# Four experts packed into three blocks of 96 slots each in a mixture-of-experts trunk kernel

## What is computed

```python
def hier_moe(h, w_rg, b_rg, w_re, b_re, w_gate, w_up, w_down):
    ...
    g_p, g_idx = lax.top_k(g_prob, 1)
    ...
    e_top, e_loc = lax.top_k(e_in, MOE_TOPK)
    e_w = jax.nn.softmax(e_top, axis=-1) * g_p
    e_id = g_idx * MOE_EXPERTS_PER_GROUP + e_loc
    ...
    def expert_block(args):
        xb, e = args
        return (jax.nn.silu(xb @ w_gate[e]) * (xb @ w_up[e])) @ w_down[e]

    ys = lax.map(expert_block, (xs, block_e)).reshape(n_slots, d)
    return jax.ops.segment_sum(ys * slot_w[:, None].astype(ys.dtype), slot_tok, num_segments=t)
```

## Time and profile before

| | |
|---|---|
| median of 3 runs | 2938.73 us (2933.47 to 2940.27) |
| the profiled execution | 2944.05 us |
| its span on the core | 2942.3 us |
| PE busy | 2503.1 us, 85% |
| DVE busy | 1228.1 us, 42% |
| ACT busy | 908.3 us, 31% |
| moved by DMA | 370.44 MB |
| mean granted TensorE clock | 0.921 of full |

### The profile page before, as it was taken

How to read it: one execution, slowest core, us unless ns; L and a number is a source line. 1 busy time by engine, 2 the same in 40 slices (tenths; PEclk the granted TensorE clock), 3 DMA queues, 4 the chain that set the end, 5 groups by cost and what they waited for, 6 DMA issues and landing times.

```text
span 2942.3 us, 30451 instructions
## 1 busy us (share of the span) xinstructions
PE 2503.1 (85%) x10356; PEld 1423.7 (48%) x10374; DVE 1228.1 (42%) x2854; ACT 908.3 (31%) x1878; POOL 195.6 (7%) x372
## 2 busy tenths in 40 slices
PE   5979999188999959999579899973889997899994
PEld 3464445155664635454335644451556645445452
DVE  4342266885551331111332514768755414211115
ACT  2131266654450201111112214765544401111112
POOL 0000021200000000000200000211000000100002
PEclk9989999599999979999779899996999997899996
DMA  6100011301000369999411001121010005699985
GB/s 222 40 29 24 32 35 38 95 2 44 1 1 9 121 254 362 369 361 371 167 59 49 7 24 38 40 81 41 2 44 1 10 22 208 243 357 371 364 305 193
DMA packets 105455, 370.44 MB, mean 126 GB/s; under 512 B 20754, under 2 KB 39912, under 8 KB 80744
## 3 DMA queue, kind: packets, MB, share of 16 engines
q1 hardware_dynamic: 91500, 318.41, 30.2%
q0 software_dynamic: 13824, 50.34, 4.5%
HBM read 304.42 MB, written 64.30 MB: 125 GB/s over the span
## 4 chain that ended last, share of the span: by engine, by line
PE 75%; DVE 13%; ACT 5%; issue 4%; DMA 1%; POOL 0%; ACTq 0%; DVEq 0%; SPq 0%; POOLq 0%
PE bank L1065 15%; PE bank L732 9%; PE bank L1082 8%; PE bank L1013 8%; PE bank L735 6%; PE bank L766 6%; PE bank L696 5%; PE bank L949 4%; PE bank L952 4%; PE bank L795 4%; PE bank L933 2%; ACT group_arena L1318 2%; PE bank L1026 1%; PE bank L1051 1%; DVE residual L2090 1%
## 5 line engine op out<-in xcount | busy, mean ns | idle before, releaser
L696 PE MATMUL bank<-ident,group_arena 128*128 128x128 f32 (+1 forms) x1200 | 201.1, 308 | 129.1 <-DVE group_arena L1537 59.8
L766 PE MATMUL bank<-group_arena 96*128 96x512 f32 (+7 forms) x384 | 165.7, 531 | 133.9 <-ACTq L1216 125.9
L732 PE MATMUL bank<-w_ring,normed_cols 128*128 128x260 f32 (+2 forms) x768 | 268.0, 511 | 0.6 <-PE bank L735 0.6
L696 PEld LDWEIGHTS bank<-ident,group_arena 128*128 128x128 f32 (+1 forms) x1200 | 149.8, 156 | 190.0 <-issue 96.1
L1082 PE MATMUL bank<-heads_cols,group_arena 128*128 128x512 f32 x512 | 231.8, 595 | 2.8 <-DVE group_arena L2050 2.8
L1065 PE MATMUL bank<-w_ring,group_arena 128*128 128x512 f32 x512 | 229.5, 602 | 3.3 <-issue 1.7
L1065 PE MATMUL bank<-normed_cols,group_arena 128*128 128x512 f32 x512 | 224.9, 592 | 0.0
L1013 PE MATMUL bank<-w_ring,heads_cols 128*128 128x512 f32 x512 | 222.6, 594 | 2.0 <-DVEq L251 2.0
L732 PEld LDWEIGHTS bank<-w_ring,normed_cols 128*128 128x128 f32 x768 | 147.0, 192 | 120.0 <-issue 112.6
L1604 DVE TENSOR_REDUCE softmax_stats<-bank 128x1 f32<-128x128 f32 (+7 forms) x192 | 145.5, 758 | 122.7 <-PE bank L771 105.6
L2050 DVE COPY group_arena<-bank 128x256 f32<-128x256 f32 x64 | 27.2, 425 | 395.3 <-PE bank L1072 395.3
(11 more groups left out here) (326 smaller groups left out, 3479.8 us busy)
## 6 DMA issues: line engine op xcount, KB each, us to landing
heads_cols<-in_expert_w_down SPq DMA_DIRECT2D x64, 1024.0 KB, 9.0
w_ring<-in_expert_w_gate SPq DMA_DIRECT2D x32, 1024.0 KB, 10.0
w_ring<-in_expert_w_up SPq DMA_DIRECT2D x32, 1024.0 KB, 14.5
normed_cols<-in_expert_w_gate SPq DMA_DIRECT2D x32, 1024.0 KB, 10.5
normed_cols<-in_expert_w_up SPq DMA_DIRECT2D x32, 1024.0 KB, 15.1
expert_rows<-group_arena SPq DMA_DIRECT2D x64, 512.0 KB, 9.2
w_ring<-in_w_in SPq DMA_DIRECT2D x6, 2048.0 KB, 8.3
expert_rows<-heads_cols SPq DMA_DIRECT2D x1, 8192.0 KB, 28.7
```

Source lines behind the costliest of these rows:

```text
L696: last = pe.transpose(bank(4 + r % 2)[0:rows, col:col + src.shape[0]], src, ident[0:src.shape[0], 0:src.shape[0]])
L732: m = pe.matmul(proj_bank(n)[:, 0:width], HT[:, k, part * P:(part + 1) * P], w, start=(k == 0), stop=(k == K - 1))
L766: m = pe.matmul(L[:, c0:c1], a["q"](h, t), a["k"](h, c0, c1), start=True, stop=not (by_choice or diagonal))
```

## The change

The slots per expert go from 128 to CAP = 96, and they no longer own a block each: four experts (a quad) fill three blocks of 128 slots. PACKED = 24 blocks replace 32. `PIECES` says which rows of each of the three blocks belong to which expert of the quad, in pieces of 64 or 32 rows at multiples of 32. `gate_up` and `down` make one matmul per piece: its stationary operand is 64 or 32 columns wide, and its output goes to the PSUM partitions of the piece. All pieces of a block write the same bank. The further blocks become OVER = 21 and take whole experts (`WHOLE`).

A slot no longer holds a token alone but a row (choice x 1024 + token). It is computed as that row minus 2048, so that an empty slot, 0, becomes row 2048, which lies outside both tables and is skipped. POOL gathers with that index and scatters the results with an indirect store to `ys_dram`, which has 2048 rows; the store by SP in slot order is gone, and so is the filling of `ys_dram` in setup. At the end SP brings the rows back with 16 plain loads of 512 KB, where POOL gathered them before. `xg`, `xgT`, `sg`, `av`, `aT` and `yb` have three buffers in place of two, and the gate/up banks are three.

```diff
+CAP = 96
+PACKED = EXPERTS * CAP // P
+MORE = (SEQ - CAP + P - 1) // P
+OVER = N_ASSIGN // (CAP + 1)
...
+NB = PACKED // QUADS
+PIECES = [[(0, 0, 64), (0, 64, 32), (1, 96, 32)],
+          [(1, 0, 64), (2, 64, 64)],
+          [(2, 0, 32), (3, 32, 32), (3, 64, 64)]]
+WHOLE = [(0, 0, P)]
...
-            sp.wait_ge(setup_zero, 1)
-            sp.dma_start(ys_dram[EXPERTS * P:, :].rearrange("(a p) d -> p a d", p=P),
-                         YT[:, 0:1, :].to_broadcast([P, SLOT_ROWS - EXPERTS, D])).then_inc(setup_dma2, 16)
...
-                        settled(sp, gu_done, e + 1)
-                        load_gu(e + NW, w)
-                        settled(sp, dn_done, e + 1)
-                        load_dn(e + NW, w)
-                        store_y(e, w % 2)
+                def quad_of(q, first=False, last=False):
+
+                    e, w0 = q * NB, q * NW
+                    if not last:
+                        settled(sp, gu_done, e + 1)
+                        load_gu(w0 + NW, 0)
+                    if not first:
+                        settled(sp, dn_done, e)
+                        load_dn(w0 + 2, 2)
+                        load_dn(w0 + 3, 3)
+                    if not last:
+                        settled(sp, gu_done, e + 2)
+                        load_gu(w0 + NW + 1, 1)
+                        settled(sp, dn_done, e + 1)
+                        load_dn(w0 + NW, 0)
+                    if not last:
+                        settled(sp, gu_done, e + 3)
+                        load_gu(w0 + NW + 2, 2)
+                        load_gu(w0 + NW + 3, 3)
+                        settled(sp, dn_done, e + 2)
+                        load_dn(w0 + NW + 1, 1)
...
+                for s in range(NB):
+                    sp.wait_ge(y_out[s], 16 * QUADS)
+                for t in range(T):
+                    for k in range(2):
+                        sp.dma_start(back[k][:, t, :],
+                                     ys_dram[k * SEQ + t * P:k * SEQ + (t + 1) * P, :]).then_inc(back_in[t], 16)
...
+                for e in range(PACKED + NB):
+                    if e < PACKED:
+                        if e >= NB:
+                            pool.wait_ge(x_turned, e - NB + 1)
+                        gather(idx_i[:, e:e + 1], e, e % NB)
+                    if e >= NB:
+                        pool.wait_ge(y_lo, e - NB + 1)
+                        pool.wait_ge(y_hi, e - NB + 1)
+                        scatter(to_i[:, e - NB:e - NB + 1], e - NB, e % NB)
...
                     for k in range(K):
-                        m = pe.matmul(bank(2 + s)[:, :], xgT[:, s, k, :], Wgu[w][:, :, k, :], start=(k == 0), stop=(k == K - 1))
+                        for w, at, rows in pieces:
+                            m = pe.matmul(gu_bank[s][at:at + rows, :], xgT[:, s, k, at:at + rows], Wgu[w][:, :, k, :],
+                                          start=(k == 0), stop=(k == K - 1))
...
                     for h in range(2):
                         for k in range(2):
-                            m = pe.matmul(bank(6 + h)[:, :], aT[:, s, k, :], Wd[w][:, k, h * HALF:(h + 1) * HALF],
-                                          start=(k == 0), stop=(k == 1))
+                            for w, at, rows in pieces:
+                                m = pe.matmul(bank(6 + h)[at:at + rows, :], aT[:, s, k, at:at + rows],
+                                              Wd[w][:, k, h * HALF:(h + 1) * HALF], start=(k == 0), stop=(k == 1))
...
-                chain(dve.tensor_copy(idx_i, bank(2)[:, 0:SLOT_ROWS]))
+                chain(dve.tensor_scalar(to_f, bank(2)[:, 0:SLOT_ROWS], float(N_ASSIGN), None, ALU.add))
+                chain(dve.tensor_scalar(from_f, to_f, float(SEQ), -float(SEQ), ALU.is_ge, ALU.mult))
+                chain(dve.tensor_tensor(idx_i, from_f, to_f, ALU.add))
+                chain(dve.tensor_copy(to_i, to_f))
                 dve.sem_inc(idx_ready, 1)
```

More of the change, by code:

```diff
@@ L224, in trunk @@
         tile_root = sem("tile_root")
-        xg_in = [sem("xg_in0"), sem("xg_in1")]
+        xg_in = [sem(f"xg_in{i}") for i in range(NB)]
         gu_in = [sem(f"gu_in{i}") for i in range(NW)]
@@ L239, in trunk @@
         y_hi = sem("y_hi")
-        y_out = [sem("y_out0"), sem("y_out1")]
+        y_out = [sem(f"y_out{i}") for i in range(NB)]
         back_in = [sem(f"back_in{t}") for t in range(T)]
@@ L1073, in turn_a, with down @@
                     m.then_inc(a_turned, 1)
-                def down(e, w, s, n):
+                def down(e, pieces, s, n):
                     pe.wait_ge(a_taken, e + 1)
-                    pe.wait_ge(dn_in[w], 16 * n)
+                    for w in sorted({w for w, _, _ in pieces}):
+                        pe.wait_ge(dn_in[w], 16 * n)
                     wait_later(pe, y_lo, e)
@@ L1089, in quad_of @@
                 def quad_of(q, first=False, last=False):
-                    for w in range(NW):
-                        e, s, nx = q * NW + w, w % 2, q * 2 + ((w + 1) // 2 + 1)
-                        gate_up(e, w, s, q + 1)
-                        finish = not (first and w == 0)
+                    for r in range(NB):
+                        e, s, behind = q * NB + r, r, (r - 1) % NB
+                        gate_up(e, PIECES[r], s, q + 1)
+                        finish = not (first and r == 0)
                         if finish:
-                            turn_a(e - 1, 1 - s)
-                        if not (last and w == NW - 1):
-                            turn_x_lo(e + 1, 1 - s, nx)
-                            turn_x_hi(e + 1, 1 - s)
+                            turn_a(e - 1, behind)
+                        if not (last and r == NB - 1):
+                            turn_x_lo(e + 1, (r + 1) % NB, q + (r + 1) // NB + 1)
+                            turn_x_hi(e + 1, (r + 1) % NB)
                         if finish:
-                            down(e - 1, (w - 1) % NW, 1 - s, q + 1 if w else q)
+                            down(e - 1, PIECES[behind], behind, q + 1 if r else q)
                 quad_of(0, first=True)
@@ L1449, in quad_of @@
                 def quad_of(q, first=False, last=False):
-                    for w in range(NW):
-                        e, s = q * NW + w, w % 2
-                        gate(e, s)
-                        if not (last and w == NW - 1):
-                            take_x(e + 1, 1 - s)
-                        if not (first and w == 0):
-                            take_y(e - 1, 1 - s, q * 2 + (w - 1) // 2)
+                    for r in range(NB):
+                        e = q * NB + r
+                        gate(e, r)
+                        if not (last and r == NB - 1):
+                            take_x(e + 1, (r + 1) % NB)
+                        if not (first and r == 0):
+                            take_y(e - 1, (r - 1) % NB, q if r else q - 1)
                 quad_of(0, first=True)
@@ L1461, in _ @@
                 quad_of(QUADS - 1, last=True)
[L1462 removed]
+                take_y(PACKED - 1, NB - 1, QUADS - 1)
                 act.wait_ge(idx_ready, 1)
@@ L2059, in quad_of @@
                 def quad_of(q, first=False, last=False):
-                    for w in range(NW):
-                        e, s = q * NW + w, w % 2
-                        if not (first and w == 0):
-                            take_a(e - 1, 1 - s)
-                        gated(e, s)
-                        if not (last and w == NW - 1):
-                            take_x(e + 1, 1 - s)
-                        if not (first and w == 0):
-                            take_y(e - 1, 1 - s, q * 2 + (w - 1) // 2)
+                    for r in range(NB):
+                        e, behind = q * NB + r, (r - 1) % NB
+                        if not (first and r == 0):
+                            take_a(e - 1, behind)
+                        gated(e, r)
+                        if not (last and r == NB - 1):
+                            take_x(e + 1, (r + 1) % NB)
+                        if not (first and r == 0):
+                            take_y(e - 1, behind, q if r else q - 1)
                 quad_of(0, first=True)
```

159 lines of the change are left out of this document (74 added, 85 removed).

## The result

The changed kernel takes 3217.24 us (3214.19 to 3218.76), the kernel before 2939.5 us on the same chip. The ratio is 1.0947, 95% interval 1.0928 to 1.0966: 278 us slower. The forecast was 3236 us.

What follows compares the result with a forecast made beforehand. PE and DMA both bound the expert loops; after the change PE would. Loops +264, layer 0's further block +31, layer 1's way back +2, the rest 0: 2938.7 + 297 = 3236 us, range 2830 to 3265 (own case 3190 to 3265).

Steps and rivals of the forecast that it cites:

- The step and the block: Expert loops on PE: each 64/32 change empties the array; mixed step 2.00 us, mixed block 25.2, equal-piece block 11.8.
- The quad: Four experts in three blocks on PE: 62.2 us against 45.7 now, +132 us per layer, +264 in all.
- the tails: From last y to combine: +31 us in layer 0 for one further block, +2 us in layer 1.
- DMA: Expert loops after the change: DMA needs 40.1 of a quad's 62.2 us at 366 GB/s and is hidden.
- both limits hold at once: Middle of the expert loops before the change: PE busy 102.00 of 102 us, DMA share 1.00 at 366 GB/s.
- rival (a): Expert loops: sizes 64, 32 and 32 stream together, DMA bounds at 40.1 us per quad; 2850 us, chance 0.36.
- (b): Expert loops: only two streams run at once, quad 45.6 us; 2972 us, chance 0.06 together with (d).
- (c): Expert loops: no overlap of column pieces at 512 columns, 93 us per quad; 3724 us, chance 0.02.
- rival (d): Expert loops: skipped rows still cost DMA time, 46 us per quad where DMA bounds; near 2972 us, chance 0.06 with (b).
- DVE's walk: End of layer 1: DVE's empty iterations, not the gathers, are late; six more cost 3 to 5 us.
- POOL's stores: Gathers and scatters issued by POOL, 2 to 3 us per block: nothing, up to 5 us per quad if scatters are dearer.
- small edits: Routing's three more DVE steps, +0.6 us per layer, and setup without its clearing, -1 us: together 0.

Runs made afterwards that it cites:

- split rows: The kernel before with each gate_up and down matmul made of row pieces: 2960.59 us for 64 and 64, 3814.04 us for 64, 32 and 32.
- the other order: The changed kernel with the 64-wide piece of each quad's third block put first at every step: 3233.48 us.
- all-32 kernel: The changed kernel with every piece 32 columns wide, four per block: 2817.77 us, ratio to the kernel before 0.9578.
- the fuller gather: The changed kernel with all pieces 32 wide and half of gate_up's steps, its gather also moving a row for each empty slot: 2798.79 us.
- half of gate_up: The changed kernel with all pieces 32 wide, gate_up making only four of its eight steps: 2784.84 us.

## Why the prediction came out right

**The step and the block** carried the sum, and they hold. That 64 to 32 empties the array was a choice from neighbouring rows, at a chance of 0.55; no row of the kernel before had such a change, and the experiments with equal pieces and with split rows now show it. A step was to be 2.00 us; it is 1.985. Of my 0.15 and 0.13 us per change, the trace has 0.14 (0.093 and 0.051) at the 64-wide piece and 0.12 (0.093, 0.025 and the 7 ns between the two starts) at the 32-wide ones. A block with mixed pieces in both operations and no help at a seam is 25.15 us (kernel before with 64, 32 and 32), where I had 25.2; the block of equal pieces is 11.77, where I had 11.8.

**The quad** was 62.2 us by the prediction and is 60.97. The term that I had left out is the seam: 32-wide pieces at the end of down and at the start of gate_up stream together. With the other order, and without that overlap, it is 62.07. The two loops therefore cost 243 us in place of 264, 21 us less; the tails took 3 us more than said, and the parts of the profile make 1 us more than the medians differ by. That is the error of 19 us.

**DMA** was hidden, as I had said, at a share of 0.57 (I had written 0.65). But its limit was wrong. I read a share of 1.00 at 366 GB/s as "both limits hold at once". 366 was only what 11.43 us per expert ask for; at the same share of 1.00 the all-32 kernel moves 419. This had no part in the forecast, but it did in rival (a), whose 2850 us would have been 2818: its bound of 40.1 us per quad should have been 36 or less.

**Rival (a)**, the streams of all sizes together, is what the kernel with equal pieces does and the changed one does not. Rivals (b) and (c) fall with the periods. Of rival (d), the fuller gather speaks against a skipped row that costs its full time; whether it costs half of it or nothing stays open, and in the forecast, where PE bounds, it has no part.

**The tails.** Layer 0: 43 us between the last y and combine predicted, 44.07 measured, by the steps that I had listed; from the loop's last y to the y of the further block it was 25.4 us, as the steps' sum, and SP's loads came 12.9 us behind the scatter. Layer 1: 12 to 17 us predicted, 14.88 measured, and +4.0 in place of +2, since the wait before was 10.84 there and not the 12.17 of layer 0. DVE's walk was late, as I had written, and not the loads: SP had issued the first pair more than 10 us ahead of combine, at 3159.09 and 3159.47.

**POOL's stores and the small edits** at nothing: PE is busy for 490.1 of 492.9 us, so no gather or scatter held it up for more than 3 us in a loop. The small edits can't be told apart: the unchanged code around them differs by up to 5 us between the two executions.

## What to carry to other kernels

Packing several small operands side by side in the stationary matrix pays only if all pieces that should stream together have the same width; cut the wide ones down to the narrowest, here four records of 32 columns cost what one of 128 does (7.05 and 7.03 us per gate_up), while each change of width costs the whole overlap and 0.12 to 0.14 us. Price a packed loop from the period of one step, seams included, before its transfers. And don't read a DMA share of 1.00 as a limit on what DMA can move: here it stood from 366 to 420 GB/s, and only a form of the kernel in which the engine waits for its data showed the limit.

## What the runs showed of the hardware that I had not expected

- Pieces of equal width in different columns stream together across operations (0.97 us hidden per quad) and across weight buffers (7.05 us for four streams, 7.03 for one). The Trainium skill, page "TensorEngine Tiling (Array Packing)", section Tiling Modes, says that a change of mode drains the array; the trace agrees for 64 and 32 columns, with 93 ns at each of the 698 changes at full clock.
- DMA's share of busy time was 1.00 to 1.02 at 366 (kernel before), 404 and 419 (all-32) and 414 and 420 GB/s (half of gate_up). The share alone did not tell what was left.
- Twenty empty iterations of a hardware loop with a condition in it held up the issue of transfers by 10 us (12.9 us behind the scatter, and 2.9 with a condition around the loop).
